# Renumbering the features so that an expert's weight block is one 8192-byte run per partition

## The reference, cut to what matters

```python
u = rmsnorm(x, ffn_norm_g).reshape(B * S, D)                       # 512 x 1024
s = sigmoid(u @ w_router)                                          # 64 experts
_, idx = top_k(where(expert_mask, s + router_bias, -inf), 8)       # 8 experts for each token
w = 2.5 * s[idx] / sum(s[idx])
for each expert e, for the tokens that chose it:                   # all 64 experts are used
    gate, up = split(u[tok] @ w_exp_up[e])                         # 1024 x 512
    acc[tok] += w * ((silu(gate) * up) @ w_exp_down[e])            # 256 x 1024
x = x + acc + swiglu(u, w_shared_up, w_shared_down)
```

## Time and profile before

| | |
|---|---|
| median of 3 runs | 1267.52 us (1266.24 to 1271.38) |
| the profiled execution | 1268.87 us |
| its span, first to last instruction | 1267.0 us |
| mean granted TensorE clock | 0.984 of 2.4 GHz |
| busy in the span | PE 1168.9, DVE 918.3, ACT 724.0, POOL 238.0 us |
| moved by DMA | 285.29 MB, mean 225 GB/s |

### The profile page before, as it was taken

The page is one execution under the profiler, slowest core; times in us unless marked ns, Lnnn a source line. Parts: engine busy times, 40 slices in busy tenths (PEclk is TensorE's granted clock), DMA queues, the critical chain, the costliest instruction groups (busy, mean ns, idle before and its releaser), DMA issues.

```text
span 1267.0 us, 17831 instructions
## 1 busy us (share of the span) xinstructions
PE 1168.9 (92%) x5911; PEld 883.1 (70%) x5911; DVE 918.3 (72%) x1343; ACT 724.0 (57%) x926; POOL 238.0 (19%) x146
## 2 busy tenths in 40 slices
PE   4999998999999899898999999999999999999993
PEld 3699987766677788565777666667666666666662
DVE  4576477544433693667999999889889888988882
ACT  7443333334333322425778777777777777777772
POOL 1000000000000000001343342333333332333331
PEclk9999998999999999899999999999999999999998
DMA  6312231212121323727999999999999999999992
GB/s 215 125 58 93 83 112 47 75 59 66 33 67 64 120 100 100 286 76 265 345 353 349 359 365 358 352 347 347 345 342 353 351 343 350 341 345 346 345 291 35
DMA packets 133357, 285.29 MB, mean 225 GB/s; under 512 B 11876, under 2 KB 34424, under 8 KB 133316
## 3 DMA queue, kind: packets, MB, share of 16 engines
q1 hardware_dynamic: 118580, 250.88, 56.0%
q0 software_dynamic: 14736, 33.87, 11.6%
HBM read 272.11 MB, written 29.38 MB: 238 GB/s over the span
## 4 chain that ended last, share of the span: by engine, by line
PE 46%; DMA 31%; DVE 9%; ACT 7%; issue 4%; SPq 1%; DVEq 0%; POOL 0%; POOLq 0%; ACTq 0%
PE bank L1370 36%; DMA arena<-in_w_exp_up_dram 16%; DMA arena<-in_w_exp_down_dram 12%; ACT split L521 5%; DVE split L1258 4%; PE bank L1538 2%; PE bank L1565 2%; DMA arena<-u_rows,arena 2%; PE bank L1449 1%; ACT arena L521 1%; PE bank L1682 1%; PE bank L1550 1%; PE bank L1701 1%; DMA arena<-in_x_dram 1%; DVE arena L944 0%
## 5 line engine op out<-in xcount | busy, mean ns | idle before, releaser
L1258 DVE TENSOR_TENSOR split<-arena,split 128x2048 fp32r<-128x2048 f32 x192 | 438.9, 2287 | 70.1 <-ACT split L521 68.8
L521 ACT ACTIVATE split<-arena 128x2048 fp32r<-128x2048 f32 x192 | 366.9, 1917 | 93.5 <-DMA arena<-in_w_exp_up_dram 76.0
L1370 PE MATMUL bank<-split,gatheredT 128*96 128x512 f32 x1536 | 374.2, 399 | 7.2 <-DVE gatheredT L1265 3.0
L1370 PEld LDWEIGHTS bank<-split,gatheredT 128*96 128x96 f32 x1536 | 244.6, 163 | 112.2 <-issue 5.8
L1370 PE MATMUL bank<-split,hidT 128*96 128x512 f32 x768 | 191.9, 398 | 1.5 <-ACT arena L521 1.5
L474 POOL DMA_INDIRECT arena<-u_rows,arena x64 | 128.4, 2007 | 251.7 <-DVE arena L1274 194.1
L1370 PEld LDWEIGHTS bank<-split,hidT 128*96 128x96 f32 x768 | 119.1, 162 | 47.0 <-issue 1.6
L482 POOL DMA_INDIRECT out_dram<-arena x64 | 101.7, 1589 | 257.7 <-ACT arena L521 180.1
L1370 PE MATMUL bank<-hT_high,front_split 128*128 128x512 f32 x448 | 143.9, 403 | 0.8 <-DVE hT_low L852 0.8
L521 ACT ACTIVATE arena<-bank 96x512 f32<-96x512 f32 (+4 forms) x217 | 107.7, 532 | 57.5 <-PE bank L1370 29.2
L1370 PEld LDWEIGHTS bank<-hT_high,front_split 128*128 128x128 f32 x448 | 81.4, 189 | 28.1 <-issue 11.5
(11 more groups left out here) (237 smaller groups left out, 1346.1 us busy)
## 6 DMA issues: line engine op xcount, KB each, us to landing
arena<-in_w_exp_up_dram SPq DMA_DIRECT2D x128, 1024.0 KB
arena<-in_w_exp_down_dram SPq DMA_DIRECT2D x64, 1024.0 KB
arena<-in_w_in_dram SPq DMA_DIRECT2D x14, 1024.0 KB, 5.5
arena<-in_w_in_dram SPq DMA_DIRECT2D x10, 768.0 KB, 4.5
arena<-in_w_branches_dram SPq DMA_DIRECT2D x4, 1024.0 KB, 5.0
arena<-in_w_out_dram SPq DMA_DIRECT2D x4, 1024.0 KB, 4.9
arena<-in_x_dram SPq DMA_DIRECT2D x4, 512.0 KB, 5.4
arena<-in_w_mem_kv_dram SPq DMA_DIRECT2D x2, 1024.0 KB, 5.2
```

What stands on the lines that cost most here:

```text
L521: return nc.scalar.activation(o, i, ACT.Copy, **kw)
L1258: v.tensor_tensor(both[:, 1], raw[q % RAW], both[:, 0].bitcast(F32), ALU.subtract).then_inc(low_done, 1)
L1370: ins = mm(bank, left[a], right[b], start=first and q == 0, stop=last and q == 2)
```

## The change

The 1024 features are given other places. Partition p now holds the weight rows 8p to 8p+7, so position k*128+f of u holds feature 8f+k. For this, second_norm writes u_tok in that order, the router's and the shared expert's weights are read with `(p k) n`, and each up block of an expert takes rows 8p+4j to 8p+4j+3, which lie together: 4 x 2048 = 8192 bytes. The 256 hidden columns are likewise written by L1294 so that position k*128+f holds column 2f+k, and the down block takes rows 2p and 2p+1, 8192 bytes. The shared expert's hidden columns keep their order. Loops, buffers, waits and the number of instructions and DMAs are the same.

```diff
-            w_sup = io["w_shared_up"][0].rearrange("(k p) n -> p k n", p=P)
+            w_sup = io["w_shared_up"][0].rearrange("(p k) n -> p k n", p=P)
...
-            sp.dma_start(w_router[:, :, :], io["w_router"][0].rearrange("(k p) n -> p k n", p=P)).then_inc(c_in[10], 16)
+            sp.dma_start(w_router[:, :, :], io["w_router"][0].rearrange("(p k) n -> p k n", p=P)).then_inc(c_in[10], 16)
...
-            up_src = io["w_exp_up"][0].rearrange("e (k p) n -> p e k n", p=P)
-            dn_src = io["w_exp_down"][0].rearrange("e (k p) (h n) -> p e k h n", p=P, n=512)
+            up_src = io["w_exp_up"][0].rearrange("e (p j k) n -> p e j (k n)", p=P, j=2)
+            dn_src = io["w_exp_down"][0].rearrange("e (p k) n -> p e (k n)", p=P)
...
                 if j < 2:
-                    sp.dma_start(raw[s], up_src[:, e, 4 * j:4 * j + 4, :]).then_inc(raw_in[s], 16)
+                    sp.dma_start(raw[s].rearrange("p k n -> p (k n)"), up_src[:, e, j, :]).then_inc(raw_in[s], 16)
                 else:
-                    sp.dma_start(raw[s].rearrange("p (k h) n -> p k (h n)", h=2),
-                                 dn_src[:, e].rearrange("p k h n -> p k (h n)")).then_inc(raw_in[s], 16)
+                    sp.dma_start(raw[s].rearrange("p k n -> p (k n)"), dn_src[:, e, :]).then_inc(raw_in[s], 16)
...
             def second_norm(t):
...
-                v.scalar_tensor_tensor(u_tok[:, t, :], x_tok[:, t, :], small[:, 12 + t:13 + t], ffn_gain, ALU.mult,
+                v.scalar_tensor_tensor(u_tok[:, t, :].rearrange("p (k f) -> p f k", k=KD), x_tok[:, t, :].rearrange("p (f k) -> p f k", k=KD),
+                                       small[:, 12 + t:13 + t], ffn_gain.rearrange("p (f k) -> p f k", k=KD), ALU.mult,
                                        ALU.mult).then_inc(u_ready, 1)
...
-                v.scalar_tensor_tensor(hid[0:ROWS, n % 2, :], e_act[0:ROWS, n % 2, :], slot_w[0:ROWS, n % 4:n % 4 + 1],
-                                       bank[0:ROWS, FH:2 * FH], ALU.mult, ALU.mult).then_inc(hid_ready, 1)
+                v.scalar_tensor_tensor(hid[0:ROWS, n % 2, :].rearrange("p (k f) -> p f k", k=2),
+                                       e_act[0:ROWS, n % 2, :].rearrange("p (f k) -> p f k", k=2), slot_w[0:ROWS, n % 4:n % 4 + 1],
+                                       bank[0:ROWS, FH:2 * FH].rearrange("p (f k) -> p f k", k=2), ALU.mult,
+                                       ALU.mult).then_inc(hid_ready, 1)
```

## The result

The changed kernel takes 1247.67 us (median of 4 runs, 1245.58 to 1252.12), the kernel before 1266.88 us in the same job. The ratio is 0.9847, 95% interval [0.9808, 0.9886]: 1.5% faster. The profiled execution took 1245.77 us, its span is 1244.0.

A forecast was written before the change was run, and what follows sets the result against it. It took expert-weight DMA to bound the kernel from about expert 9. 0.40 us for 60 experts gave 24 us, less 2 for late meetings; 1268.87 - 22 = 1246.9, median adjustment to 1246 us; 8-in-10 range 1228 to 1274.

The forecast's parts named there:

- a front in which nothing had been expected: Before the experts: reordered router and shared-block loads, with some 30 us of cover for the shared blocks, would change nothing.
- Runs whole, about 60,000 packets: Hardware queue q1: if 8 KB runs travel as one packet each, its packets fall from 118580 to about 60,000.
- Saving of 0.40 us an expert: Expert weight loads: longer runs cut the period from 10.53 to 10.13 us, for 60 experts, 24 us.
- the upper of the two fits: Expert loads: packet times fitted in the expert stage gave 0.61 us less per expert, the front's fit 0.32, for whole packets.
- Windows with q1 alone at 410 to 426 GB/s: Sign of being right: short windows where only the hardware load queue moves would run at this rate.
- The early experts keep the engines' pace: Experts 1 to 9 stay at 9.85 us each; the stock of loaded blocks lasts longer, so their saving isn't lost.
- L1294 still 477 ns: DVE's product writing the 256 hidden columns in steps of 128 words would cost nothing extra.
- the upper bound of 193: Strided write at L1294: at most 193 ns on top of 477, lifting the engines' pace to 10.04 us, under 10.13.
- ACT's waits for the expert weights near 40 us: Sign of being right, expert stage: ACT's waits for weights fall to near 40 us instead of 89.
- Rival D: Long packets hold up the gather: 1.6 us more a turn, 5.7 us to spare; if decisive 1297 us; chance 0.08.
- A: Expert loads: bytes alone set the rate, so no gain: 1267 us, or 1262 at the edge; chance 0.22.
- C: Expert loads: the new addresses, runs 16 KB apart, are slower: 1285 us at the slowest rate; chance 0.12.

The follow-up runs named there:

- e3: Changed kernel with each up block taking every second row, in 2048-byte runs, down still 8192: 1269.75 us, 1.0021 of the kernel before.
- e5: Changed kernel with up blocks in 4096-byte runs (two rows of every four), down still 8192: 1261.60 us, 0.9951 of the kernel before.
- e4: Changed kernel with DVE reading the row selection before its first remainder, so the gather is issued earlier: 1249.32 us, 0.9856 of the kernel before.
- e7: Changed kernel with DVE writing in order, PE's transposes reading in steps, and the gather issued earlier: 1249.14 us, 0.9855 of the kernel before.
- e1: Changed kernel's loads alone: DVE writes in order, router rows in old order, features mismatched: 1255.27 us, 0.988 of the kernel before.
- e6: Changed kernel with DVE writing in order and PE's transposes picking the columns in steps, same output: 1260.28 us, 0.9948 of the kernel before.
- e11: Changed kernel with every scatter row index out of bounds, so scatters add nothing: 1226.87 us, 0.9698 of the kernel before.
- e2: Kernel before with only the strided writes and new router row order, old expert loads, features mismatched: 1267.83 us, 1.0005 of the kernel before.
- e9: Changed kernel with each up block again one unbroken megabyte, runs still 8192 bytes: 1253.99 us, 0.9917 of the kernel before.

## Why the prediction came out as it did

The forecast of 1246 us missed the measured 1247.67 by 1.7. Its mechanism, that longer packets load faster, was at work (e3, e5); what it said of the rest of the stage was not: the gathers, and not the loads, are what PE waits for in the changed kernel. That the total came so close is in part luck, since misses cancel. Where 22 us were forecast, the later experts gave 25.2, the early ones took 4.3 back, and 1.9 came from a front in which nothing had been expected. By its steps:

- **Runs whole, about 60,000 packets:** 59,572.
- **Saving of 0.40 us an expert:** 0.47 from expert 9 on, 0.33 on the mean of the 63 periods (658.14 / 63 = 10.45 before, 637.16 / 63 = 10.11 after). With the gathers out of the way (e4, e7), where the loads bound as the text had it, the period is 10.13 and 10.14, which is the 10.13 of the forecast. From 680 to 1200 us the median packet of q1 takes 86 ns at 2 KB, 162 at 4 KB and 312 at 8 KB, so 64 x 86 + 16 x 162 - 24 x 312 = 0.61 us less for an expert, the upper of the two fits. Why no more than 0.39 to 0.47 of it reaches the period isn't shown.
- **Windows with q1 alone at 410 to 426 GB/s:** taken over 1 us at every 0.5 us from 680 to 1200, and only where the DMA share is 0.97 or more, they average 395 GB/s before (339 windows) and 416 after (119). In e4 and e7, with the same loads, they average 412; in e1 and e6 398, in e3 394, e5 405. Without the condition on the share they are 393 before (349 windows) and 404 after (154), which is under the forecast. The direction holds, but e1 and e6 show that such windows alone would not settle it; e3 and e5 do.
- **"The early experts keep the engines' pace":** this step failed. They went from 9.85 to 10.40 us. From 590 to 680 us PE waits 6.5 + 4.0 us for gathered rows, where the first of the two was 1.8 before; in e11, whose scatters move no data, the early period is 9.88. Part of what the later experts gained was given back here, +4.3 us.
- **"L1294 still 477 ns":** failed, 680 to 692 ns, and 2048 for 1285 in second_norm. Of the two bounds the lower was taken because L1244 is a write alone and seemed to show no cost; beside a one-input step (294 ns) it shows some 0.41 ns an element, and the measured cost is 203 to 215 ns, above the upper bound of 193. It cost the sum nothing (e2, e11) beyond some 3 us of DVE work ahead of the router, where the path as a whole came out no later.
- **"ACT's waits for the expert weights near 40 us":** failed, none. Rival D's wait stood in their place, 30.7 + 9.2 us at L1703, and hid them; e4 brings 36.5 us of them back.
- **Rival D:** its price for a turn, 1.6 us, was measured as 0.7 on the mean and 1.2 in one turn, and its slack was wrong, 1.1 us and not 5.7, because a burst was given to the wrong DMA. A second cause, POOL's longer instruction beside L1258, stood in no sum: 0.8 us of the lag. Late rows came about in nearly every expert and yet did not decide, since they cost the kernel hardly more than the late weights beneath them. In e6 they take some 10 to 13 us of the gain.
- **A and C:** ruled out, A by e3 to e5 and the ratio, C by e3 and e9.

Open: why writes in order, which shorten DVE's work, leave PE waiting longer for gathered rows (e6, and the trace of e1); why e3 gains nothing from its down loads; what makes single experts late, and with that the spread of the change; and what a gather issued outside L1258 would be worth, which no run tried.

## What to carry to other kernels

Where the DMA engines are full, lengthen the runs: from 2 and 4 KB to 8 KB gave 0.47 us in 10.5 here, for one strided write that lay in slack. Before counting on such a gain, follow a small transfer of the other queue from its issue to its use, and find its packets by counting bursts back from the last one; packets that move right after an issue can belong to the DMA before. Compare the same transfer in both kernels, since two gathers differ in their rows. When one wait vanishes and another of its size appears, two limits lie close together, and only an experiment that relieves both shows the floor.

## What I had not expected of the hardware

- **The software queue's lag has two parts.** The first is POOL's own instruction: 0.96 to 1.37 us, or, where DVE's remainder (L1258) runs as it starts, until 0.85 us after L1258's end. The second is from its end to the first packet: 0.7 us in the quiet case below, where q1 is empty (first packet at 580.6, q1 moving only from 582), and 3.2 on the mean of the busy stage. Together they make 1.7 to 2.0 us in quiet and 4.5 to 6.0 with q1 full in the changed kernel, 2.8 to 6.2 in the kernel before. That q1's load makes the second part longer is read from these stages; it wasn't tried apart. In the quiet case of the changed kernel L1258 starts behind POOL:

```profile
578.95 0.96 POOL L473 DMA_INDIRECT arena<-u_rows,arena  x1 [23.03 <-DVE arena L1274]
579.07 4.49 DVE L1258 TENSOR_TENSOR split<-arena,split 128x2048 fp32r<-128x2048 f32 x2 [0.57 <-ACT split L520]
```

- **A strided write costs by its step.** 512-byte steps add 0.75 to 0.84 ns an element to a two-input product; 16-byte steps add some 0.4 to a step of one input, if L1244's 398 ns may be held against L1232's 294.
- **An empty scatter is nearly free for the DMA engines.** With all rows out of bounds its 112 packets start within 1.2 us on the mean, where they took 3.4; one of them takes 1.1% of the engines' time in 5.5 us.
